# Moving the rotation of the S5 input matrix from GpSimd to VectorE in a two-block transformer kernel

## The reference

```python
u, z = jnp.split(h @ w_in, 2, axis=-1)
ug = u.reshape(B_, L, SSM_GROUPS, SSM_GROUP)            # 128 groups of 16 channels, 64 states each
bu_re = jnp.einsum('blgc,gnc->blgn', ug, bb_re)
bu_im = jnp.einsum('blgc,gnc->blgn', ug, bb_im)
x_re, x_im = scan(a_re, a_im, bu_re, bu_im)             # x[t] = a * x[t-1] + bu[t], complex
y = einsum(x_re, c_re) - einsum(x_im, c_im) + d_skip * ug
y = jax.nn.gelu(y);  y = y * jax.nn.sigmoid(y @ w_glu + b_glu)
out = (y * jax.nn.silu(z)) @ w_out
```

## Time and profile before

| | us |
|---|---|
| three runs | 3326.32, 3318.86, 3324.22 (median 3324.22) |
| the profiled execution's own time | 3326.32 |
| its span in the profile | 3324.5 |
| TensorE busy | 3208.9 (97%) |
| VectorE busy | 2210.9 (67%) |
| ScalarE busy | 1494.1 (45%) |
| GpSimd busy | 119.3 (4%), of which `turned` has 53.4 |

### The profile page before, as it was taken

One profiled execution on the slowest core, in us unless ns is written; L12 is line 12 of the kernel. 1 busy time (PEld: TensorE's weight loads), 2 busy tenths in 40 slices (PEclk: granted clock), 3 DMA queues, 4 the chain that ended last, 5 costly groups with the idle time before them and its releaser, 6 DMA issues.

```text
span 3324.5 us, 57535 instructions
## 1 busy us (share of the span) xinstructions
PE 3208.9 (97%) x21222; PEld 2868.7 (86%) x21222; DVE 2210.9 (67%) x2849; ACT 1494.1 (45%) x2001; POOL 119.3 (4%) x143
## 2 busy tenths in 40 slices
PE   7999999999999998999999999799999999999998
PEld 7898889887878887999889997699997989888876
DVE  5876888665766665454675458999865555677765
ACT  6443433454434445444343333656534533455553
POOL 0000000000000000000000000344100000000000
PEclk9999999999999999999999999899999999999999
DMA  6865777446767774555785568344455466644435
GB/s 221 280 241 196 269 283 251 167 157 221 278 236 269 269 255 163 183 182 181 267 305 183 182 223 315 112 150 145 140 177 183 151 228 249 227 146 146 146 125 179
DMA packets 191445, 688.42 MB, mean 207 GB/s; under 512 B 21904, under 2 KB 26256, under 8 KB 189968
## 3 DMA queue, kind: packets, MB, share of 16 engines
q1 hardware_dynamic: 183744, 669.07, 58.5%
q10 hardware_dynamic: 7504, 16.56, 1.4%
HBM read 683.45 MB, written 2.10 MB: 206 GB/s over the span
## 4 chain that ended last, share of the span: by engine, by line
PE 84%; DVE 11%; ACT 2%; DMA 2%; issue 1%; ACTq 0%; DVEq 0%; SPq 0%
PE psum L672 43%; PE psum L655 33%; DVE ring_parts L1874 3%; PE psum L715 1%; DVE work L2097 1%; DMA ring<-in_stream 1%; DVE arena_high L2102 1%; PE psum L818 1%; PE psum L750 1%; PE psum L682 1%; DVE arena_high L2103 1%; PE psum L702 1%; PE psum L742 1%; PE psum L724 1%; DVE work L2059 1%
## 5 line engine op out<-in xcount | busy, mean ns | idle before, releaser
L1874 DVE TENSOR_TENSOR ring_parts<-ring,hi_parts 128x1024 fp32r<-128x1024 f32 x1002 | 1186.5, 1221 | 386.6 <-ACT hi_parts L1116 376.4
L1116 ACT ACTIVATE hi_parts<-ring 128x1024 fp32r<-128x1024 f32 x1002 | 1024.7, 1056 | 668.4 <-DMA ring<-in_stream 653.5
L655 PE MATMUL psum<-arena_low_parts,hi_parts 128*128 128x256 f32 x6048 | 1122.5, 286 | 1.9 <-DVE ring_parts L1874 1.9
L655 PEld LDWEIGHTS psum<-arena_low_parts,hi_parts 128*128 128x128 f32 x6048 | 956.6, 193 | 14.1 <-issue 9.9
L655 PE MATMUL psum<-arena_low_parts,ring_parts 128*128 128x256 f32 x3088 | 879.0, 285 | 0.0
L672 PE MATMUL psum<-hi_parts,arena_high_parts 128*128 128x512 f32 x2304 | 759.2, 395 | 7.8 <-DVE ring_parts L1874 7.8
L672 PE MATMUL psum<-hi_parts,arena_low_parts 128*128 128x512 f32 x2112 | 696.5, 396 | 12.6 <-DVE ring_parts L1874 5.5
L655 PEld LDWEIGHTS psum<-arena_low_parts,ring_parts 128*128 128x128 f32 x3088 | 597.3, 193 | 0.0
L672 PEld LDWEIGHTS psum<-hi_parts,arena_high_parts 128*128 128x128 f32 x2304 | 434.4, 189 | 100.9 <-DVE ring_parts L1874 9.0
L672 PEld LDWEIGHTS psum<-hi_parts,arena_low_parts 128*128 128x128 f32 x2112 | 401.8, 190 | 99.4 <-issue 8.4
L672 PE MATMUL psum<-ring_parts,arena_low_parts 128*128 128x512 f32 x1216 | 477.6, 393 | 0.0
(11 more groups left out here) (325 smaller groups left out, 2257.4 us busy)
## 6 DMA issues: line engine op xcount, KB each, us to landing
ring<-in_stream SPq DMA_DIRECT2D x1272, 512.0 KB, 3.9
arena_high<-in_mem ACTq DMA_DIRECT2D x2, 1024.0 KB, 5.8
arena_high<-in_x ACTq DMA_DIRECT2D x1, 2048.0 KB, 11.9
arena_low<-in_x ACTq DMA_DIRECT2D x1, 2048.0 KB, 7.7
arena_high<-in_ssm_bc ACTq DMA_DIRECT2D x64, 32.0 KB, 2.4
arena_high<-in_ssm_bc ACTq DMA_DIRECT2D x16, 128.0 KB, 3.2
out<-arena_low SPq DMA_DIRECT2D x4, 512.0 KB, 3.6
arena_high<-in_decay ACTq DMA_DIRECT2D x1, 1024.0 KB, 8.5
```

Source lines behind the costliest of these rows:

```text
L655: mm = pe.matmul(bank[:, half:half + S], r32(w[:, slot, cols]), r32(x[part][:, k, :]), start=(k == 0 and n == 0), stop=(k == KT - 1 and n ...
L1116: act.activation(r32(hi[:, g % RING, cols]), ring[:, g % RING, cols], ACT.Copy).then_inc(hi_made, 1)
L1874: dve.tensor_tensor(r32(slot), slot, as32(hi[:, g % RING, cols]), ALU.subtract).then_inc(cut_done, 1)
```

## The change

`turned` is issued by VectorE instead of GpSimd. On VectorE it is called once before the loop of chunks, once inside the first chunk behind `direct_block(0)`, and then at the end of every chunk for the chunk after the next. GpSimd keeps the w work, and its `turned(0)` ahead of the first w work is gone. The semaphores and the values waited for are the same, and `ssm_ab_ready` is raised by VectorE.

```diff
+            def turned(cc):                      # in the VectorE program
+                dve.wait_ge(*emptied(prep_bank(cc)))
+                if cc >= 2:
+                    dve.wait_ge(ssm_in_done, cc - 1)
+                for k in range(2):
+                    did(dve.tensor_tensor(ab_tmp[:, k, :, :], ssm_b(cc), a_rows[:, k, :].unsqueeze(1).broadcast_to([P, 2, P]),
+                                          ALU.mult))
+                did.wait()
+                did(dve.tensor_tensor(turned_b[cc % 2][:, 0, :], ab_tmp[:, 0, 0, :], ab_tmp[:, 1, 1, :], ALU.subtract))
+                dve.tensor_tensor(turned_b[cc % 2][:, 1, :], ab_tmp[:, 0, 1, :], ab_tmp[:, 1, 0, :],
+                                  ALU.add).then_inc(ssm_ab_ready, 1)
...
             fractions(0)
+            turned(0)
             steps(BEFORE_S5)
...
                 direct_block(cc)
+                if cc == 0:
+                    turned(1)
                 if later:
                     fractions(cc + 1)
...
                 cut(POS[("unit", "sz", cc)] + LEAD)
+                if cc + 2 < SSM_CHUNKS:
+                    turned(cc + 2)
...
-            def turned(cc):                      # in the GpSimd program: the same body with pool,
...                                               # and a wait for its own ssm_ab_ready at its end
-            turned(0)
             for cc in range(SSM_CHUNKS):
...
                 pool.wait_ge(ssm_w_ready, cc + 1)
-                if cc + 1 < SSM_CHUNKS:
-                    turned(cc + 1)
```

More of the change, by code:

```diff
@@ L2169, in _ @@
                 did.wait()
-            def turned(cc):
[L2173 to L2183, removed]
-            turned(0)
             for cc in range(SSM_CHUNKS):
```

## The result

The change makes the kernel slower: 3340.73 us (median of 12) against 3319.09 for the kernel before in the same sessions, a ratio of 1.006 with a 95% interval of 1.0048 to 1.0074. The ratio makes it 19.9 us, the difference of the two medians 21.6; 18.6 were forecast, and 3343 us as the time. The profiled execution has a span of 3337.7 us.

The account below looks back on a forecast made before the run. TensorE was taken to bound a steady chunk at 16.33 us; VectorE out of step adds 17.6 and the start 1.0, +18.6 on 3324.2, giving 3343 us. Own range 3334 to 3350; 8 in 10: 3319 to 3350.

Parts of the forecast that it names:

- TensorE is the bound of a steady chunk, at 16.33: S5 loop: TensorE's input matmuls come every 16.33 us and set the pace; VectorE is full partly from blocked time.
- chunk 0's wait: Chunk 0: TensorE waited 3.75 us for late `back(0)`, then ran at a lower clock; the change would win 5.3 us.
- VectorE's own work, 15.7 with 1.16 for the rotation: Each steady chunk: VectorE's own 14.55 us plus 1.16 for `turned`'s four instructions become 15.7 us.
- In step it would cost nothing: Steady chunk: VectorE needs 15.7 + 0.39 = 16.1 us, under TensorE's 16.33, with 0.2 us to spare.
- Out of step a full w work costs 2.5: Late chunks: w work beside the cuts and `turned` blocks VectorE 2.5 us (bounds 0.39 and 3.5), making 18.2 a chunk.
- my row: Chunk 0 of the kernel before: L2103 took 1.54 us instead of 0.69 beside the w work, 0.85 per L2192.
- The pattern: From chunk 1 on: TensorE's waits repeat every three chunks, 53.4 us or 17.8 each; `back(14)` ends 17.6 us later.
- The start: Ahead of the loop: added `turned(0)`, freed blocked time and w work beside L1472 sum to +1.0 us, from -0.6 to +1.9.
- The time of 3343 us: Whole kernel: 17.6 + 1.0 = +18.6 us put on the median of three runs, 3324.2.
- rival C: Loop: VectorE late but blocked 1.5 instead of 2.5 us, 17.2 a chunk; +11, 3335 us; within out of step's 0.65.
- B: Loop in step, the first wait only moves to chunk 1: between -1 and +2, 3325 us; chance 0.15.
- A: Loop: VectorE gets into step once, after the first wait and lower clock; not slower, -4.3, 3320 us; chance 0.17.

Follow-up runs that it names:

- two runs in which one block of known size was left: Changed kernel with the rotation behind direct_block in every chunk, 3322.81 us; changed kernel with GpSimd's w work waiting for the rotation, 3322.05 us.
- two edited kernels: Changed kernel with the rotation ahead of the cuts, 3326.01 us; changed kernel without w work in chunks 2 to 6 and chunk 8's scans made twice, 3326.59 us.
- the delayed kernel: Changed kernel with the w work left out in chunks 2 to 6 and the scans of chunk 8 made twice; 3326.59 us, ratio 1.0022 to the kernel before.

## Why the prediction was right

- *TensorE is the bound of a steady chunk, at 16.33.* Right: 16.34 in every run in step, and a stage 5.1 to 5.4 shorter than before once chunk 0's wait is gone, where 5.3 had been forecast for that wait.
- *VectorE's own work, 15.7 with 1.16 for the rotation.* Right: 1.19 measured for the rotation, and 15.7 + 0.86 = 16.6 and 15.7 + 0.55 = 16.3 are the beats of two runs in which one block of known size was left.
- *In step it would cost nothing.* Shown by the w work left out in chunks 2 to 8, a state that then holds by itself. The 0.2 us to spare are not there, though: the w work costs some 0.6 in that state and not 0.39 (L2101 behind it takes 0.96 instead of 0.41), and VectorE then needs 16.3 of the 16.34.
- *Out of step a full w work costs 2.5.* It was 2.7 and 2.8, and 1.6 (not 2.1) in the first chunk behind a long wait. By the exclusive lock of the Trainium skill (SBUF — State Buffer, section SBUF: two separate sides) it would have been 3.5; the trace lies between this rule and my row, nearer to the row.
- *The pattern.* Forecast: a wait, a chunk without a loss, one with most, one with all, 53.4 us for three chunks, 17.8 each. Measured: 71.7 for four, 17.9 each, since the smaller first loss (1.6, not 2.1) lets `back` end 1.3 us ahead of the handover two chunks behind the wait, instead of 0.6, and puts the next wait off by one chunk. The first wait came in chunk 1, as written, with 3.6 us (3.0 forecast). That the means agree so well is partly luck: a wait comes less often than forecast and costs more, 6.3 us beyond four times 16.34 instead of 4.4 beyond three times 16.33.
- *The start*, +1.0: between 0.4 and 1.2 in the two profiles of the changed kernel, too small to be told apart by times.
- *The time of 3343 us* lies nearer to 3340.73 than its terms do. The loss was 21.6 by the medians instead of 18.6, and the kernel before had been taken at 3324.2, the median of three runs, where twelve give 3319.09. The two errors partly cancel. In the paragraph on rival C, 13 chunks of 0.9 and the start are +12.7 and not +11, which would put that end at 3337.
- *Rivals.* B and C did not come. That a run may come into step by a long step of TensorE stands in A as "once, after the first wait and lower clock", and is what single executions of two edited kernels showed. The changed kernel's own executions spread from 3316 to 3348, which would fit A for the fast ones; this is not shown, since both of its profiled executions, at 3339.5 and 3342.9, stayed out of step.
- GpSimd is slower at this work, as the Trainium skill's GPSIMD Engine Reference (section Engine selection) says, and the trace agrees: the two products take 0.74 on VectorE and 1.71 on GpSimd. The move still loses, because of where the four instructions now stand.

What stays open: what sets the length of the stretch at the lower clock, 3.4 or 6.8 us behind waits of 3.1 to 3.8 us, which by the rows above goes with whether an execution comes into step.

## What to carry to other kernels

When two engines block each other, as GpSimd and VectorE do here on instructions with two operands in SBUF, the price of an operation is set by what runs beside it. Before moving work, look at what the other engine's operations are released by, and put those that don't collide (here the ones that read PSUM) right behind that release. A loop with two engines near their limits can have two ways of running; compare the slack ahead of the release with the work that stands there, and order the other engine with a semaphore where it doesn't fit.

## What the runs showed of the hardware

Two pieces of the same work, 1.16 us of four short instructions and 2.27 of two long ones, make a difference of 13 us by the ratios (1.0060 against 1.0021) according to which stands last. That a GpSimd operation gets in only between instructions, so that short ones give it more openings, would explain it and is not shown by itself. What a late w work takes from VectorE is 2.7 to 2.8 us for operations that take 3.5 alone. And behind the same wait of 3.25 us TensorE ran at 1.2 GHz for 6.8 us in one execution of the delayed kernel and for 3.4 us in the other. The slower TensorE here works for the kernel: it moves the next handover back and lets VectorE catch up.
